# Three of four MLP down projections of each layer by Strassen's scheme with seven half-size products

## The reference

```python
h = rms_norm(x, norm_mlp[l])
x = x + jnp.square(jax.nn.relu(h @ w_mlp_in[l])) @ w_mlp_out[l]   # w_mlp_in 1024 x 4096, w_mlp_out 4096 x 1024
```

## Time and profile before

| what | value |
|---|---|
| three runs, device time | 3752.54, 3754.1 and 3754.1 us, median 3754.1 us |
| the profiled execution, device time | 3749.64 us |
| its span | 3748.3 us |
| PE busy | 3604.7 us (96%), 17428 matmuls |
| DVE busy | 2111.5 us (56%) |
| ACT busy | 1327.1 us (35%) |
| POOL busy | 1194.4 us (32%) |
| mean granted clock of PE | 0.984 |
| DMA | 291.86 MB, mean 78 GB/s |

### The profile page before, as it was taken

How to read it: one execution, slowest core, us unless ns; L and a number is a source line. 1 busy time by engine, 2 the same in 40 slices (tenths; PEclk the granted TensorE clock), 3 DMA queues, 4 the chain that set the end, 5 groups by cost and what they waited for, 6 DMA issues and landing times.

```text
span 3748.3 us, 43619 instructions
## 1 busy us (share of the span) xinstructions
PE 3604.7 (96%) x17428; PEld 2771.2 (74%) x17428; DVE 2111.5 (56%) x2942; ACT 1327.1 (35%) x2226; POOL 1194.4 (32%) x486
## 2 busy tenths in 40 slices
PE   8889999988999999999999999999999999999998
PEld 6547888854688877576777688887767777778887
DVE  6987564788755555623463674455543355375444
ACT  6353122535411132544333431122344433442112
POOL 0003444100344442132323244444123232334443
PEclk9989999998999999999999999999999999999999
DMA  4102333310233342021222133334112222223332
GB/s 135 46 6 74 97 99 96 91 51 12 62 96 96 97 144 67 29 79 56 79 62 73 58 94 97 98 98 147 43 46 68 68 74 62 68 74 96 96 96 84
DMA packets 80793, 291.86 MB, mean 78 GB/s; under 512 B 9648, under 2 KB 11088, under 8 KB 80080
## 3 DMA queue, kind: packets, MB, share of 16 engines
q1 hardware_dynamic: 77808, 278.03, 24.5%
q10 hardware_dynamic: 2784, 11.03, 0.9%
HBM read 284.84 MB, written 2.10 MB: 77 GB/s over the span
## 4 chain that ended last, share of the span: by engine, by line
PE 85%; DVE 10%; issue 2%; ACT 2%; DMA 0%; SPq 0%; DVEq 0%; ACTq 0%
PE acc L337 24%; PE acc L339 23%; PE acc L338 23%; PE banks L657 2%; PE banks L608 2%; PE banks L987 2%; PE banks L640 2%; DVE conv_c L1406 1%; DVE QK L900 1%; DVE stat L744 1%; PE banks L1741 1%; PE banks L1004 1%; DVE near L926 1%; DVE gap L888 1%; DVE pair L409 1%
## 5 line engine op out<-in xcount | busy, mean ns | idle before, releaser
L281 POOL TENSOR_TENSOR w_lo<-w_raw,w_hi 128x1024 fp32r<-128x1024 f32 x482 | 1194.2, 2478 | 2526.9 <-ACT w_hi L234 2526.9
L234 ACT ACTIVATE w_hi<-w_raw 128x1024 fp32r<-128x1024 f32 x518 | 548.9, 1060 | 1726.1 <-PE acc L339 1652.7
L337 PE MATMUL acc<-hH,w_hi 128*128 128x512 f32 x1776 | 729.1, 411 | 11.8 <-DVE sig L2129 6.6
L339 PE MATMUL acc<-hL,w_hi 128*128 128x512 f32 x1776 | 699.3, 394 | 0.0
L338 PE MATMUL acc<-hH,w_lo 128*128 128x512 f32 x1776 | 699.0, 394 | 0.0
L337 PEld LDWEIGHTS acc<-hH,w_hi 128*128 128x128 f32 x1776 | 337.7, 190 | 97.6 <-issue 25.6
L337 PE MATMUL acc<-H,w_hi 128*128 128x512 f32 x1024 | 400.4, 391 | 3.8 <-DVE L L401 3.8
L337 PE MATMUL acc<-midH,w_hi 128*128 128x512 f32 x1024 | 400.9, 391 | 0.3
L372 DVE TENSOR_TENSOR xT<-acc,xT 128x512 f32<-128x512 f32 x160 | 110.6, 691 | 513.4 <-PE acc L339 501.0
L338 PE MATMUL acc<-midH,w_lo 128*128 128x512 f32 x1024 | 398.6, 389 | 0.0
L339 PE MATMUL acc<-midL,w_hi 128*128 128x512 f32 x1024 | 398.6, 389 | 0.0
(11 more groups left out here) (338 smaller groups left out, 4601.5 us busy)
## 6 DMA issues: line engine op xcount, KB each, us to landing
w_raw<-in_stream SPq DMA_DIRECT2D x518, 512.0 KB, 3.5
cw<-in_cmpw ACTq DMA_DIRECT2D x2, 2048.0 KB, 7.2
mixed<-in_cmpw ACTq DMA_DIRECT2D x2, 2048.0 KB, 12.6
x_tok<-in_x SPq DMA_DIRECT2D x2, 1024.0 KB, 7.2
out<-probsT SPq DMA_DIRECT2D x4, 512.0 KB, 4.0
stack<-Z ACTq DMA_DIRECT2D x8, 128.0 KB, 2.3
stack<-Z ACTq DMA_DIRECT2D x8, 127.8 KB, 2.4
C<-in_consts SPq DMA_DIRECT2D x1, 640.0 KB, 10.0
```

Source lines behind the costliest of these rows:

```text
L234: act.activation(w_hi[:, u % WB, 0:w], w_raw[:, u % 2, 0:w], ACT.Copy).then_inc(hi_split, 1)
L281: pool.tensor_tensor(w_lo[:, u % WB, 0:w], w_raw[:, u % 2, 0:w], w_hi[:, u % WB, 0:w], ALU.subtract)\
L337: pe.matmul(acc[n % 2][:, :], wh, H[:, k, :], start=(k == 0), stop=False)
L339: last = pe.matmul(acc[n % 2][:, :], wh, Lo[:, k, :], start=False, stop=(k == nk - 1))
```

## The change

In the blocks b = 0, 1, 2 of every layer (12 blocks in all) the down product is made by the Winograd form of Strassen's scheme. Now 128 tokens of the activations are stationary and 512 columns of the weights move, so the result comes out by rows of tokens and is gathered in a tile `rows`, which is turned back and added to `xT` during the up tiles of block 3. Block 3's own down product is made as before.

- The activations `mid` (1024 hidden x 512 tokens, uncut in `hidden_rows`) and the 1024 x 1024 weights are four quarters each. Four sums of quarters on each side (`x_sum`, `w_sum`) and seven products `A11, A12, S1, S4, S2, S3, A22` of half size give the result.
- A product is two weight units ("halves") of 12 matmuls each: 2 groups of 128 tokens x 2 blocks of 128 hidden features x 3. So a block has 14 units of 12 matmuls in place of 8 of 24.
- A block's weights come as eight loads of 512 KB into a tile `quads` (`load_quad`), which lies where `hH` and `hL` lie; they are issued by SP between the loads of the up units 3 to 7. ACT and POOL cut all 14 units, out of `quads`, into the same three buffers `w_hi`, `w_lo`.
- DVE makes the sums in place, ACT casts each of the seven left operands to `XH` (`high_act`), DVE subtracts for `XL` (`low`), and DVE adds each finished product out of PSUM to `rows` (`take`, 14 of 128 x 512). `hidden` goes from four DVE instructions per up tile to two (`part`) in blocks 0 to 2.
- `S4` is accumulated in the same PSUM banks on top of `S1`, and `S2`, `S3`, `A22` on top of `A11`: PE waits with the later one until DVE has taken the earlier (`product_taken`).
- `rows` is set to zero once a layer (`memset` of 128 x 4096), and PE turns it back with 32 transposes of 128 x 128 a layer (`rows_back_pe`).

The diff, cut to its core:

```diff
+PRODUCTS = ("A11", "A12", "S1", "S4", "S2", "S3", "A22")
+X_SLOT = dict(A11=0, A12=1, S1=2, S4=3, S2=0, S3=1, A22=2)
+PRODUCT_BANK = dict(A11=0, A12=2, S1=4, S4=4, S2=0, S3=0, A22=0)
+OPENS = ("A11", "A12", "S1")
-FF_GROUPS = [g for b in range(FB) for g in ((f"up{b}", [(8, 1)] * 8), (f"down{b}", [(8, 1)] * 8))]
+FF_GROUPS = [g for b in range(FB - 1) for g in ((f"up{b}", [(8, 1)] * 8), (f"mul{b}", [(2, 0)] * MULS))]
+FF_GROUPS += [(f"up{FB - 1}", [(8, 1)] * 8), (f"down{FB - 1}", [(8, 1)] * 8)]
...
+                            for i in {3: (0,), 4: (1,), 5: (2,), 6: (3,), 7: (4, 5, 6, 7)}.get(at, ()):
+                                load_quad(layer, b, i)
...
+        def products_pe(g, layer, b, XH, XL):
+            for i, name in enumerate(PRODUCTS):
+                pe.wait_ge(x_low, len(PRODUCTS) * g + LOW_ORDER.index(name) + 1)
+                for half in range(HALVES):
+                    u = FIRST_MUL[layer, b] + HALVES * i + half
+                    wait_lo(pe, u)
+                    for t in range(2):
+                        if half == 0 and name not in OPENS:
+                            before = [x for x in PRODUCTS[:i] if PRODUCT_BANK[x] == PRODUCT_BANK[name]][-1]
+                            pe.wait_ge(product_taken, MULS * g + taken_after(before) - 1 + t)
...
+                        for kk in range(2):
...
+                            pe.matmul(bank, xh, wh, start=(name in OPENS and k == 0), stop=False, skip_group_check=True)
+                            pe.matmul(bank, xl, wh, start=False, stop=False, skip_group_check=True)
+                            last = pe.matmul(bank, xh, wl, start=False, stop=ends, skip_group_check=True)
...
+        def rows_back_pe(layer, k, rows):
...
+            for t in range(NT):
+                last = pe.transpose(B[1 + k % 2][:, t * P:(t + 1) * P], rows[:, t, k * P:(k + 1) * P], ident)
+            last.then_inc(rows_turned, 1)
...
+        HIGH_AT = {0: "A12", 1: "S1", 2: "S2", 3: "S4", 5: "S3", 7: "A22"}
...
+                for m in range(MULS):
+                    if m in HIGH_AT:
+                        high_act(g, HIGH_AT[m], parts, XH)
+                    split_hi(FIRST_MUL[layer, b] + m + WB)
...
+            dve.memset(rows[:, :, :], 0.0)
...
+            def part(i, a, free, value):
+                z = mid[:, i, :]
+                dve.scalar_tensor_tensor(z, a[:, :], 0.0, rstd[:, :], ALU.max, ALU.mult).then_inc(up(free), 1)
+                dve.wait_ge(free, value)
+                dve.tensor_tensor(z, z, z, ALU.mult).then_inc(mid_made, 1)
...
+                    if k == NK - 1:
+                        w_sum(g, b, "S1", 0)
+                    ups.evacuate(part, 1)
+                    if k == 3:
+                        x_sum(g, "S3", "A11", "A21", ALU.subtract)
+                    if k == 5:
+                        low(g, "A11")
...
+                x_sum(g, "S1", "A21", "A22", ALU.add)
+                low(g, "A12")
+                w_sum(g, b, "S1", 1)
+                x_sum(g, "S2", "S1", "A11", ALU.subtract)
+                low(g, "S1")
+                x_sum(g, "S4", "A12", "S2", ALU.subtract)
+                take(g, "A11")
+                low(g, "S2")
+                low(g, "S4")
+                w_sum(g, b, "S2", 0)
+                w_sum(g, b, "S2", 1)
+                take(g, "S1")
+                take(g, "A12")
+                low(g, "S3")
+                w_sum(g, b, "S3", 0)
+                w_sum(g, b, "S3", 1)
+                low(g, "A22")
+                take(g, "S4")
+                w_sum(g, b, "A22", 0)
+                w_sum(g, b, "A22", 1)
+                take(g, "S2")
+                take(g, "S3")
+                take(g, "A22")
...
+            for k in range(NK):
+                ups.evacuate(hidden, 1)
+                dve.wait_ge(rows_turned, NK * layer + k + 1)
+                dve.tensor_tensor(xT[:, k, :], B[1 + k % 2][:, :], xT[:, k, :], ALU.add).then_inc(rows_taken, 1)
```

More of the change, by code:

```diff
@@ L94, in plan_units, with mul_of @@
                 j += 1
-    return units, first_tile
-UNITS, FIRST_TILE = plan_units()
+    return units, first_tile, first_mul, quads_at
+UNITS, FIRST_TILE, FIRST_MUL, QUADS_AT = plan_units()
+def mul_of(u):
+    layer, _, group, _, _, _ = UNITS[u]
+    if not group.startswith("mul"):
+        return None
+    b = int(group[3:])
+    return layer * (FB - 1) + b, u - FIRST_MUL[layer, b]
+RANK = []
+for _u in range(len(UNITS)):
+    RANK.append((RANK[-1] if RANK else -1) + (mul_of(_u) is None))
+BY_RANK = [u for u in range(len(UNITS)) if mul_of(u) is None]
 def ranges(kind, qt):
@@ L477, in mlp_pe, with parts_of @@
                     behind(k)
[L479 to L484, removed]
+        def parts_of(mid, spare):
+            first, second = slice(0, T // 2), slice(T // 2, T)
+            return dict(A11=mid[:, 0:4, first], A12=mid[:, 4:8, first], A21=mid[:, 0:4, second], A22=mid[:, 4:8, second],
+                        S1=mid[:, 0:4, second], S2=mid[:, 0:4, first], S4=mid[:, 4:8, first],
+                        S3=spare[:, :, :].rearrange("p a (h t) -> p (a h) t", h=2))
@@ new lines, in high_act @@
+        def high_act(g, name, parts, XH):
+            slot = X_SLOT[name]
+            if name in ("A11", "A12", "A22"):
+                act.wait_ge(mid_made, NK * g + (4 if name == "A11" else NK))
+            else:
+                act.wait_ge(x_summed, 4 * g + ("S3", "S1", "S2", "S4").index(name) + 1)
+            before = [x for x in PRODUCTS[:PRODUCTS.index(name)] if X_SLOT[x] == slot]
+            if before:
+                act.wait_ge(product_ready, MULS * g + HALVES * (PRODUCTS.index(before[-1]) + 1))
+            elif g:
+                before = [x for x in PRODUCTS if X_SLOT[x] == slot]
+                act.wait_ge(product_ready, MULS * (g - 1) + HALVES * (PRODUCTS.index(before[-1]) + 1))
+            act.activation(XH[:, slot, :, :], parts[name], ACT.Copy).then_inc(x_high, 1)
@@ L485, in mlp_act @@
+        HIGH_AT = {0: "A12", 1: "S1", 2: "S2", 3: "S4", 5: "S3", 7: "A22"}
+        def mlp_act(layer, gains, y, sq, XH, mid, spare, side=None, last=None):
+            parts = parts_of(mid, spare)
+            for b in range(FB - 1):
+                g = layer * (FB - 1) + b
+                ups = Group(layer, f"up{b}")
                 for k in range(NK):
-                    ahead.split_ahead(1)
+                    ups.split_ahead(1)
+                    if k == 4:
+                        high_act(g, "A11", parts, XH)
@@ L511, in hidden @@
                 dve.tensor_tensor(midL[:, i, :], r, midH[:, i, :], ALU.subtract).then_inc(up(mid_ready), 1)
[L512 to L520, removed]
+            ups = Group(layer, f"up{FB - 1}")
+            for k in range(NK):
+                ups.evacuate(hidden, 1)
+                dve.wait_ge(rows_turned, NK * layer + k + 1)
+                dve.tensor_tensor(xT[:, k, :], B[1 + k % 2][:, :], xT[:, k, :], ALU.add).then_inc(rows_taken, 1)
+            down = Group(layer, f"down{FB - 1}")
+            dve.wait_ge(rows_taken, NK * (layer + 1))
             add_and_scale(2 * layer + 2, down, y, hH, hL, sq, layer < LAYERS - 1)
@@ L1515, in on_vector @@
                     out_dve(layer, yt, H2, L2, pair)
-                    mlp_dve(layer, midH, midL, pair_r, yt, pair, None if layer else angles_dve)
+                    mlp_dve(layer, midH, midL, XH, XL, hidden_rows, rows, pair_r, yt, pair, None if layer else angles_dve)
                 on_sync()
@@ L2324, in mlp_units, with quarters @@
 def mlp_units(up, down):
-    return [u for b in range(FB) for u in cut(up[:, :, b * D:(b + 1) * D]) + cut(down[:, b * D:(b + 1) * D])]
+    units = []
+    for b in range(FB):
+        rows = down[:, b * D:(b + 1) * D]
+        units += cut(up[:, :, b * D:(b + 1) * D]) + (quarters(rows) if b < FB - 1 else cut(rows))
+    return units
+def quarters(w):
+    half = D // 2
+    return [tiles(w[:, k * half + i * half // 2:k * half + (i + 1) * half // 2, n * half:n * half + half], 2, half)
+            for k, n in ((0, 0), (1, 0), (0, 1), (1, 1)) for i in range(HALVES)]
 def cut(w):
```

191 lines of the change are left out of this document (160 added, 31 removed).

## The result

The changed kernel takes 3924.33 us (median of 4 runs, 3922.92 to 3927.14), the kernel before 3754.1: a ratio of 1.0456, 95% interval 1.0442 to 1.0471, so 170 us slower. The forecast was 3937 in a range of 3830 to 3985.

What follows compares the result with a forecast made beforehand. PE was taken to bound the kernel before; after the change, POOL and DVE taking turns at SBUF decide. Port +130.4 (matmul savings included), turning back +14.1, clock +38.4 sum to +182.9 on 3749.6; with 4.5 for the median, 3937, range 3830 to 3985.

Steps and rivals of the forecast that it cites:

- Matmuls: PE in the product blocks: 168 in place of 192 matmuls at 0.2267 us, -5.44 us a block, -65.3 over 12.
- The port: Product phase: POOL's cuts and DVE's two-operand SBUF instructions take turns whole; phase 54.7 against 43.83 us, +130.4 over 12 blocks.
- The way: POOL's and DVE's shared access to SBUF, held by 16 DVE instructions and 15 cuts for 51.0 us a product phase.
- The clock: PE at 1.2 GHz after three waits a block: 3.2 us lost a block, +38.4 in all, between 19 and 115.
- the 4.5 us added for the median: Whole kernel: the runs' median lies 4.5 us above the profiled execution, so 3932.5 becomes 3937.
- Turning back: Up tiles of block 3: four transposes between matmuls cost 0.44 us a group, 8 groups x 4 layers, +14.1 us.
- The `memset`: DVE zeroing 4096 columns once a layer: 4.8 us, hidden, so zero; at most 7 us in all.
- Loads: Weight loads all in the up half, 16 in 43.5 us at 193 GB/s: hidden, zero cost.
- Signs: Profile after: L690, L685, L703 mean 2 to 2.5 us, takes 0.69, PE waiting for takes and `XL`, clock pieces of 3.4.
- No turns: Rival: DVE and POOL work side by side in the product phase, -52 us, 3702; chance 0.08.
- Well packed: Rival: port full but DVE's takes in time, phase 51.0 us, 3855, up to 3880; chance 0.14.
- Clock and queue worse: Rival: 6.8 us at the low clock after each wait, 4014, or loads late in the up half; chance 0.09.

Runs made afterwards that it cites:

- run 2: Changed kernel with DVE's low parts and sums in product phases of blocks 1 and 2 over 128 columns, POOL's cuts whole: 3773.63 us, ratio 1.006.
- run 4: Changed kernel with idle matmuls before PE's waits: 9 before A12, 25 before S4, 19 before S3: 3897.99 us, ratio 1.0395.
- run 5: Changed kernel with one in place of four transposes for each of the 32 turned tiles: 3915.57 us, ratio 1.0435.
- run 1: Changed kernel with POOL's cut of each product-phase weight unit made over 128 of its 1024 columns: 3711.99 us, ratio 0.990.
- run 7: Changed kernel with POOL's cuts of product-phase weight units replaced by a memset of the same 1024 columns: 3708.76 us, ratio 0.9882.
- run 3: Changed kernel with only DVE's order altered, takes of S1, S4 and S2 moved ahead of other work: 3871.77 us, ratio 1.0321.
- run 8: Changed kernel, whole computation, DVE cutting 7 of 14 weight units, two weight sums moved to the up phase, takes earlier: 3758.33 us, ratio 1.0015.
- run 9: Kernel of run 8 with unit 10 in place of 11 cut by DVE, S1 and S3 weight sums earlier, ACT's casts later: 3760.55 us, ratio 1.0023.
- run 10: Kernel of run 9 with 8 idle matmuls before PE's wait for A12: 3752.5 us, ratio 1.0004.

## Why the prediction was right, point by point

**Matmuls.** 168 at 0.2267 are 38.1, as run 2's phases of 38.08 show. Exchanging the moving and the stationary operand costs nothing. No phase of any run was shorter.

**The port.** Worked forward it was 54.7 us a phase without the clock's loss; run 4 has 54.85. The waits fell where the working put them, before A12, S4 and S3, the one before S4 the longest: 2.9, 6.9 and 5.7 us in run 4, where 3.0, 7.0 and 5.5 were worked out. In the first block of the changed kernel, with the clock low, they are 2.9, 6.2 and 4.1. The slower matmuls fill a part of them. The way's 51.0 us counted 15 cuts; 14 fell into the phase, and it was in use for 49.5.

**The clock.** The term that was off in size: 3.2 us a block forecast, 2.3 measured (57.14 - 54.85), 27 us in place of 38. I had taken the loss after the last wait as uncovered and half of that after the first two; the half was a guess between bounds. The stretches at low clock were not shorter than assumed but longer. In the first block they stand at the three waits (columns as in the earlier trace rows):

```profile
389.30:392.60 3.30, 3.19 (x8) 2.52 (x9) 3.30 (x3) 0.00 (x0) 2.27 (x1) 0.50 0.00 0
406.40:413.10 6.70, 4.94 (x12) 3.91 (x13) 6.25 (x8) 0.75 (x1) 2.42 (x1) 0.50 0.00 0
426.90:430.10 3.20, 3.20 (x9) 2.55 (x8) 0.00 (x0) 0.04 (x1) 0.16 (x1) 0.50 0.00 0
```

Some 27 matmuls at a pitch near 0.43 in place of 0.227 lose about 5.5 us there (4.8 was assumed), but only 57.09 - 54.85 = 2.2 lengthen the phase: more of the loss lay under DVE's lateness than the 1.6 assumed. So the size came out near in part because two errors stood against each other. The 11 us too much in this term, less the 1.8 and 0.9 too little in the port and the turning back, make the forecast 8 us too high; the rest of the 13 between 3937 and 3924 is mostly the 4.5 us added for the median, which lay only 1.1 above the profiled execution in the changed kernel.

**Turning back.** 14.1 forecast, 15.0 measured (4 x 3.75); 0.111 a transpose (run 5).

**The `memset`.** Thought to take 4.8 us and to hide: it takes 3.47 and hides, the first up phase is 45.63 before and 45.66 after. **Loads:** hidden; 191 GB/s in the up phases with PE busy in all of them.

**Signs.** L690 has a mean of 2.48 us over its 84 (2.69 for the 72 shown) and L703 of 2.38, near the 2 to 2.5 named. L685, named with them, has half of its 48 at 1.21 (sums S2 and S4 mostly meet no cut), mean 2.26. The tails of both sides, 3.43 for DVE (3.3 was named as the most) and 3.41 for POOL, are close to one whole instruction of the other and one's own (2.40 + 1.22 = 3.62, less 0.2). The takes kept 0.69. PE waited for takes and for `XL`, and not for POOL's cuts. The clock at 0.50 came in pieces of 3.4 us, as named, and of 6.8.

**The rivals.** "No turns" fell with runs 1, 2 and 7: the instructions with two operands in SBUF do wait. "Well packed", 3855, was what a better order could reach with POOL doing all cuts; run 3 came to 3872. It lacked mainly DVE's order, so its mechanism, a floor set by the way, is borne out, at 49.5 us in place of 51, and its small chance suited the order as written. "Clock and queue worse" foresaw stretches of 6.8 us at low clock, and they came, but most of their loss was covered; the loads hid. The saving that the change was after, 65 us, is real on PE: runs 1 and 7 are 1.0 to 1.2% faster than the kernel before, and leave out most of what is contended for.

## What to carry to other kernels

Fewer matmuls pay only if the elementwise work that makes their operands fits into the time that is left; count it by the resource it holds, not by engine, for two engines at 78% and 67% of a phase (44.4 and 38.5 us of 57.1) looked far from full, while the way between them was in use for 49.5 us of the 57.1, and each instruction on it waited for the other engine's. Instructions of DVE with two operands in SBUF and POOL's reading ones excluded each other whole here (1.22 us became up to 3.43, 2.40 up to 3.41), so price each pair as a sum, move a cut to the engine that holds the way for less (by the prediction's estimate 1.1 us in place of 2.3), and put the takes on which PE waits in front of the work that can be blocked. A wait of PE can cost a second time through the clock: in the changed kernel the granted clock was 0.50 around or after every wait before S4 and S3 (3.8 to 6.9 us) and after ten of the twelve before A12 (2.9). It was so even after the 2.0 us wait of run 8 in six of its twelve phases, though nothing was lost there: they are 43.03 to 43.07 us long, and those at full clock 43.03 to 43.33. What such a stretch costs depends on how late the next thing is that PE waits for. Idle matmuls within the wait got back 26 us here (run 4).

## What the runs showed that I had not expected

- POOL's `memset` of 1024 columns takes 0.96 us and neither waits for DVE's two-operand instructions nor delays them, where POOL's subtraction of the same size is held up to 3.41 us.
- DVE's `memset` of 128 x 4096 floats takes 3.47 us, 0.85 ns a column, against 1.19 for a subtraction.
- In run 9 four of the six phases of the first two layers were 1.1 to 1.3 us longer than all others; with 1.8 us of idle matmuls in the wait before A12 (run 10) they were not. The trace shows what differed: in those four the granted clock was at 0.50 for 6.8 us after the wait, in the others for 3.4 or not at all.

```profile
393.80:400.50 6.70, 6.06 (x14) 4.79 (x15) 6.49 (x7) 2.60 (x4) 2.53 (x1) 0.50 0.00 0
482.50:485.90 3.40, 3.40 (x9) 2.62 (x9) 3.19 (x4) 1.27 (x2) 1.98 (x1) 0.50 0.00 0
```

Phases at full clock have a wait of 1.4 us before S1, which the slower matmuls of the others fill. It covers the loss of 3.4 us at half rate (about 1.5) and not that of 6.8 (about 2.8). Why the stretch was longer in those four stays open.
